# A two-layer streaming encoder step on one core: layer C's channel projection for two tiles at once with split operands, and taps behind the scan in every second unit

## The reference, cut to what matters

```python
h = rms_norm(x, rms_g)                       # x * rsqrt(mean(x*x)) * g
z, xbc, dt = _split(h @ w_in, SPLIT_C)       # 2048, 3072 and 32 columns
xbc, new_conv = causal_conv(xbc, conv_state, conv_w, conv_b)   # 4 taps along the rows, per channel
xbc = jax.nn.silu(xbc.astype(F32))
xs, Bm, Cm = _split(xbc, (D_INNER_C, G_C * N_C, G_C * N_C))
y, S = ssd_scan(xs, Bm, Cm, dt, A, S0)       # chunked scan, state carried from chunk to chunk
y = y + d_skip[..., None] * xs
y = y.reshape(B, L, G_C, D_INNER_C // G_C) * jax.nn.silu(z)
y = rms_norm(y, g_y) ; return x + y @ w_out, S, new_conv
```

## Time and profile before

| what | before |
|---|---|
| median of 3 runs | 3149.06 us (3145.97 to 3149.65) |
| the profiled execution | 3149.56 us, span 3147.8 us |
| granted TensorE clock, mean | 0.974 |
| busy: PE, DVE, ACT | 2924.8, 1870.8, 1411.4 us |
| layer C (1250 to 2764 us of the span): PE, DVE, ACT busy | 1451.5, 1225.1, 802.6 us |

### The profile page before, as it was taken

How to read it: one execution, slowest core, us unless ns; L and a number is a source line. 1 busy time by engine, 2 the same in 40 slices (tenths; PEclk the granted TensorE clock), 3 DMA queues, 4 the chain that set the end, 5 groups by cost and what they waited for, 6 DMA issues and landing times. The chain is left out here.

```text
span 3147.8 us, 50003 instructions
## 1 busy us (share of the span) xinstructions
PE 2924.8 (93%) x18074; PEld 2485.2 (79%) x18074; DVE 1870.8 (59%) x4798; ACT 1411.4 (45%) x2901; POOL 67.9 (2%) x167
## 2 busy tenths in 40 slices
PE   6999996888888986899999999999999999889999
PEld 3798985676766764799988999799997999768787
DVE  3344444444444443588887888788887888832322
ACT  3555555333333332355555555555554555431211
POOL 0000001000000000000000000000000000000000
PEclk9999998999999998899999999999999999889999
DMA  5122223122222211521214221322223212154343
GB/s 191 70 86 85 85 85 134 59 72 85 85 84 85 84 65 56 183 62 57 66 51 132 67 66 56 90 89 67 67 63 104 60 58 67 44 187 141 126 140 114
DMA packets 147547, 280.86 MB, mean 89 GB/s; under 512 B 46231, under 2 KB 69274, under 8 KB 143226
## 3 DMA queue, kind: packets, MB, share of 16 engines
q1 hardware_dynamic: 145458, 274.12, 26.5%
q10 hardware_dynamic: 1992, 5.48, 0.4%
HBM read 204.29 MB, written 75.26 MB: 89 GB/s over the span
## 5 line engine op out<-in xcount | busy, mean ns | idle before, releaser
L2065 PEld LDWEIGHTS bank<-hT_c,w_group 128*128 128x128 f32 x6528 | 750.0, 192 | 39.7 <-issue 34.0
L2065 PE MATMUL bank<-hT_c,w_group 128*128 128x128 f32 x6528 | 751.3, 275 | 0.0
L1889 DVE SCALAR_TENSOR_TENSOR conv_acc<-u,convw,conv_acc 128x128 f32<-128x128 f32 (+1 forms) x1224 | 331.1, 338 | 10.4 <-ACT conv_acc L1823 8.0
L2052 PE MATMUL bank<-wz_high,h_high 128*128 128x512 f32 (+1 forms) x544 | 240.0, 441 | 12.9 <-DVE wz_low L1970 12.9
L2290 PE MATMUL bank<-wout_high,yT_high 128*128 128x512 f32 (+1 forms) x544 | 212.4, 390 | 6.6 <-DVE wout_low L2259 6.6
L2052 PE MATMUL bank<-wz_low,h_high 128*128 128x512 f32 (+1 forms) x544 | 215.9, 397 | 0.0
L2052 PE MATMUL bank<-wz_high,h_low 128*128 128x512 f32 (+1 forms) x544 | 215.5, 396 | 0.0
L2290 PE MATMUL bank<-wout_high,yT_low 128*128 128x512 f32 (+1 forms) x544 | 212.3, 390 | 0.0
L2290 PE MATMUL bank<-wout_low,yT_high 128*128 128x512 f32 (+1 forms) x544 | 212.2, 390 | 0.0
L710 PE MATMUL bank<-wa_high,hT_high 128*128 128x512 f32 (+5 forms) x544 | 189.6, 349 | 12.1 <-DVE wa_low L567 12.1
L710 PE MATMUL bank<-wa_low,hT_high 128*128 128x512 f32 (+5 forms) x544 | 186.8, 343 | 0.0
(11 more groups left out here) (289 smaller groups left out, 5815.1 us busy)
## 6 DMA issues: line engine op xcount, KB each, us to landing
hT_c<-h1T SPq DMA_DIRECT2D x64, 512.0 KB, 3.3
acb<-acT SPq DMA_DIRECT2D x64, 512.0 KB, 3.3
yT_in<-yT SPq DMA_DIRECT2D x32, 1024.0 KB, 5.1
yT<-yT_t SPq DMA_DIRECT2D x64, 256.0 KB, 3.5
xin<-in_x_prompt SPq DMA_DIRECT2D x16, 512.0 KB, 3.7
h0T_high_d<-hT_high SPq DMA_DIRECT2D x16, 512.0 KB, 2.6
h0T_low_d<-hT_low SPq DMA_DIRECT2D x16, 512.0 KB, 3.5
h0T_high<-h0T_high_d SPq DMA_DIRECT2D x16, 512.0 KB, 3.5
```

Source lines behind the costliest of these rows:

```text
L1889: ins = V.scalar_tensor_tensor(acc[:, i, 0:R], ub[:, i, tap:tap + R], c["convw"][:, tap * CT + ct:tap * CT + ct + 1], acc[:, i, 0:R], ALU. ...
L2052: ins = M(B_Z[0:x.R, :], h[:, k, 0:x.R], wt[:, k, :], start=(k == 0 and p == 0), stop=(k == KT - 1 and p == 2))
L2065: ins = M(out, wg[x.g % 2][:, k, j * P:(j + 1) * P], hT[x.buf][:, k, :], start=(k == 0), stop=(k == KT - 1))
```

## The change

Layer C's channel projection (x, B and C blocks) is made for a pair of prompt tiles at once. Its operands are split like those of the gate: three fp32r matmuls with 256 moving columns for each block of channels and of the inner dimension, instead of two f32 matmuls with 128 moving columns (one for each tile). The pair's six blocks ("slots": B, C, x0, x1, x2, x3) are made in two halves of three: a unit with an even t makes slots 0 to 2 of the next pair, a unit with an odd t makes slots 3 to 5 of its own pair. The sample's 32 rows ride with the first pair (288 columns). Taps, first tap, tanh and the SiLU product work on three slots of 256 (or 291) columns in each unit that has a half. In units with odd t (and in the sample's) VectorE makes them before the scan, as before; in units with even t the scan comes first and the taps behind it. Units with t = 1 have no half.

h of layer 1 is written by SWA as a high and a low part, without `rms_g`; `rms_g` is multiplied into the weights when they are split. So `low` and ACT's high part of h leave layer C, and in their place both the x/B/C weights (8 blocks of 768 columns) and z's weights (8 of 512) are split for each group, at the ends of the steps of tiles 14 and 15. ACT's half of z goes away: VectorE reads z from PSUM. In SWA the prompt's bias is restored once by a DMA instead of by a GpSimd copy for each tile.

```diff
@@ SWA
-                    V.tensor_tensor(h1T[:, 4 * k:4 * k + 4, 0:R], B_H2[k]..., bc(c["vec"][:, V_RMS1 + 4 * k:...], R), ALU.mult).then_inc(s["h2_half"], 1)
+                    V.tensor_copy(h1T[:, 4 * k:4 * k + 4, 0:R], B_H2[k]...).then_inc(s["h2_copied"], 1)
+                since(dve, s["hT_out"], x, 1, 32)
+                for k in range(2):
+                    dve.wait_ge(s["h2_high"], 2 * t + k + 1)
+                    V.tensor_tensor(h1l[:, 4 * k:4 * k + 4, 0:R], h1T[...], h1h[...].bitcast(F32), ALU.subtract).then_inc(s["h2_half"], 1)
+            def x1_high(x):
+                    A(h1h[:, 4 * k:4 * k + 4, 0:x.R], h1T[:, 4 * k:4 * k + 4, 0:x.R], ACT.Copy).then_inc(s["h2_high"], 1)
+                if x.fixed and x.t == 1:
+                    sp.wait_ge(s["sc_added"], 8)
+                    sp.dma_start(bias[:, :, 0:P], d["bprev"]).then_inc(s["bprev_in"], 16)
@@ layer C, TensorE
-                for j in (range(4), range(4, 6))[part]:
-                    out = (B_X, B_BC)[part][:, (j % 4) * P:(j % 4 + 1) * P]
-                    for k in range(KT):
-                        ins = M(out, wg[x.g % 2][:, k, j * P:(j + 1) * P], hT[x.buf][:, k, :],
-                                start=(k == 0), stop=(k == KT - 1))
+            def slot(h, i, out):
+                col = SLOT_W[i]
+                for k in range(KT):
+                    if h.first and i == 0:
+                        pe.wait_ge(s["x_low"], KT * h.g + k + 1)
+                    for p, (y, wt) in enumerate(((hh, xh), (hh, xl), (hl, xh))):
+                        ins = M(out, wt[:, k, col:col + P], y[h.par][:, k, h.h0:h.h0 + h.n], start=..., stop=...)
+                elif part == 0:
+                    slot(h, h.lo, B_U[0][:, 0:2 * P])
+                    slot(h, h.lo + 1, B_U[0][:, 2 * P:4 * P]).then_inc(s["uj_full"], 2)
+                else:
+                    slot(h, h.lo + 2, B_U[1][:, 0:2 * P]).then_inc(s["uj_full"], 1)
-                done(pe, s["xc_made"], cur)
+                pe.wait_ge(s["xc_made"], cur.halves)
@@ layer C, VectorE
             def step(cur, nxt, prv):
+                h = cur.half
+                now = h is not None and h.lo > 0
                 if prv is not None:
                     heads_sum(prv)
                 decays(cur)
-                V.scalar_tensor_tensor(zs[0:R, :], zt[0:R, :], 1.0, zh[0:R, :], ALU.add, ALU.mult)
                 if prv is not None:
                     variance(prv)
-                conv(cur, (2,))
+                if now:
+                    taps(h, (2,))
                 if prv is not None:
                     norm(prv)
-                conv(cur, (1, 0))
-                V.scalar_tensor_tensor(acc[:, :, 0:R], th[:, :, 0:R], 1.0, acc[:, :, 0:R], ALU.add, ALU.mult).then_inc(s["xc_made"], 1)
-                    low(following(nxt))
+                if now:
+                    taps(h, (1, 0))
+                    activated(h)
                 if prv is not None:
-                    turned(prv, two_before(prv))
-                scan(cur, prv)
-                    weights_low(nxt.g + 1)
+                    turned(prv, earlier(prv))
+                scan(cur, prv, nxt)
+                if h is not None and not now:
+                    taps(h, (2, 1, 0))
+                    activated(h)
+                    if nxt.t == NT - 2:
+                        weights_low(nxt.g + 1)
+                    if nxt.t == NT - 1:
+                        gate_weights_low(nxt.g + 1)
+            def taps(h, which):
+                for tap in which:
+                    for i in h.slots:
+                        y = acc[h.par][:, i, h.c0:AW]
+                        ins = V.scalar_tensor_tensor(y, ub[:, i, h.c0 + tap:AW + tap], c["convw"][...], y, ALU.mult, ALU.add)
+            def activated(h):
+                dve.wait_ge(s["x_tanh"], h.v + 1)
+                V.scalar_tensor_tensor(y, th[:, :, h.c0:AW], 1.0, y, ALU.add, ALU.mult).then_inc(s["xc_made"], 1)
+            def gate(x):                       # called in scan, ahead of the addition that waits for sup_full
+                V.scalar_tensor_tensor(z, z, 1.0, B_Z[0:x.R, :], ALU.add, ALU.mult).then_inc(s["zs_made"], 1)
@@ layer C, ScalarE: order in a step
-                first tap (6 x 128), ..., tanh(cur), high(h), tanh and half of z(nxt), copies to u(nxt)
+                first_tap(cur.half) (3 x 256), ..., tanh(cur.half) if odd t, tanh of z(nxt), copies to u(nxt.half), tanh(cur.half) if even t
```

More of the change, by code:

```diff
@@ L1176, in scores @@
                 nk = P + R
-                since(dve, s["bias_set"], x, 1)
                 since(dve, s["pt_full"], x, 1, 2)
+                if not x.sample:
+                    dve.wait_ge(s["bias_set"], 1)
+                if not x.fixed or x.t > 1:
+                    dve.wait_ge(s["bprev_in"], 16)
                 if x.sample:
@@ L1582, in layer_c @@
         xd = sb("xd", [P, GW])
-        zh = sb("z_half", [P, GW])
-        zt = sb("z_tanh", [P, GW])
-        zs = sb("zs", [P, GW])
+        zs = [sb(f"zs{i}", [P, GW]) for i in range(2)]
         yb = sb("yb", [P, GW])
@@ L1612, in __init__ @@
                 self.R = DEC if self.sample else P
-                self.buf = (g + (t if isinstance(t, int) else odd)) % 2
-                self.st_before = 19 * g + (1 if self.sample else t + 2)
[L1618 to L1624, removed]
+                self.buf = (g + ph) % 2
+                self.par = 0 if self.sample or ph in (1, 2) else 1
+                second = ph % 2 == 0
+                self.off = 0 if self.sample else UP - 3 + P * second
+                self.hoff = 0 if self.sample else (0 if self.par else DEC) + P * second
+                self.halves = 16 * g + (2 if self.sample else t if second else t + 1)
+                self.half = None
+                if self.sample:
+                    self.half = Half(g, 16 * g + 1, 1, True, 0)
+                elif self.last:
+                    if g + 1 < GC:
+                        self.half = Half(g + 1, 16 * g + 16, 0, True, 0)
+                elif not (isinstance(t, int) and t == 1):
+                    self.half = Half(g, 16 * g + t, ph % 2, False, 1 if ph in (2, 3) else 0)
+                self.st_before = 19 * g + (1 if self.sample else t + 2)
         def done(eng, sem, x, n=1):
@@ L1629, in done, with earlier @@
                 eng.wait_ge(sem, n * (x.u + 1))
+        def earlier(x):
+            if x is None or x.sample and x.g == 0:
+                return None
+            return Unit(x.g - 1, NT - 1, 0) if x.sample else Unit(x.g, x.t - 1, (x.ph + 3) % 4)
         def steps(eng, start, step, end):
-            start(Unit(0, 0))
+            start(Unit(0, 0, 0))
             for g in range(GC):
[L1636 to L1643, removed]
@@ L1644, in steps @@
-            end(Unit(GC - 1, NT - 1))
+                step(Unit(g, 0, 0), Unit(g, 1, 1), Unit(g - 1, NT - 1, 0) if g else None)
+                step(Unit(g, 1, 1), Unit(g, 2, 2), Unit(g, 0, 0))
+                with eng.Fori(2, 7, 4) as t:
+                    for i in range(4):
+                        step(Unit(g, t + i, (2 + i) % 4), Unit(g, t + i + 1, (3 + i) % 4), Unit(g, t + i - 1, (1 + i) % 4))
+                for t in range(10, NT - 1):
+                    step(Unit(g, t, t % 4), Unit(g, t + 1, (t + 1) % 4), Unit(g, t - 1, (t - 1) % 4))
@@ new lines, in load_tile, with load_pair @@
+            def load_tile(par, col, t, R):
+                for dst, src in ((hh, d["h1h"]), (hl, d["h1l"])):
+                    sp.dma_start(dst[par][:, :, col:col + R].bitcast(F32),
+                                 src[t].rearrange("p (k r) -> p k r", k=KT)[:, :, 0:R]).then_inc(s[f"h_in{par}"], 16)
+            def load_pair(t, par, first):
+                if first:
+                    load_tile(par, 0, 0, DEC)
+                for i in range(2):
+                    load_tile(par, (0 if par else DEC) + P * i, t + i, P)
@@ new lines, in _, with fresh, turned @@
+            tail = lambda k, lo, hi, ct: c["tails"][:, k, :, ct:ct + hi - lo].rearrange("p j c -> p c j")
+            def fresh(g, odd):
+                for lo, hi, ct in parts(g, odd):
+                    copy(ub[:, lo:hi, 0:3], c["convs"][:, :].rearrange("p (j c) -> p c j", j=3)[:, ct:ct + hi - lo, :])
+                nc.gpsimd.memset(ub[:, 3 * odd:3 * odd + 3, DEC + 3:UP], 0.0).then_inc(s["tail_set"], 1)
+            def turned(v, odd):
+                pool.wait_ge(s["conv_made"], v + 1)
+                pool.sem_inc(s["pool_step"], 1)
@@ new lines, in carry @@
+            def carry(odd):
+                copy(ub[:, 3 * odd:3 * odd + 3, DEC + 3:UP], ub[:, 3 * odd:3 * odd + 3, UW - 3:UW]).then_inc(s["tail_set"], 1)
+            for odd in range(2):
+                fresh(0, odd)
+            for g in range(GC):
+                for odd in range(2):
+                    turned(16 * g + odd, odd)
+                    for lo, hi, ct in parts(g, odd):
+                        copy(tail(0, lo, hi, ct), ub[:, lo:hi, DEC:DEC + 3])
```

(33 more changed lines are left out.)

409 lines of the change are left out of this document (218 added, 191 removed).

## The result

The changed kernel takes 3234.97 us (median of 4 runs, 3233.64 to 3236.84) where the kernel before takes 3149.36 us (4 runs, 3145.97 to 3150.16): a ratio of 1.0274, 95% interval 1.0257 to 1.0292. It is slower by 86 us, as forecast; 3208 was forecast, with 3150 to 3240 as the range. The profiled execution has a span of 3231.7 us against 3147.8, so the traces stand 83.9 us apart.

The account below looks back on a forecast made before the run. TensorE bounds the kernel (busy 93%), with VectorE's chain only 1.0 us to spare. From 3149.56, +13.6 (units, group edges, start), +2 (SWA) and +44 (lost clock) give 3209, so 3208 us; range 3150 to 3240.

Parts of the forecast that it names:

- TensorE's part: Layer C's projection: new matmuls at 0.1169 us pitch save 2.29 us per unit; even units take 18.58 us.
- The odd unit: Odd t in layer C: VectorE's single chain makes TensorE stand 4.8 us; next state update at T+23.38.
- The rival of cheap taps: VectorE keeps up: a tap with 256 columns costs nearly as little as with 128 (0.26 us); 3118 us; chance 0.12.
- The clock: TensorE's idling in odd units lowers its clock: 1.73 us lost in nine of ten of 28 units, 44 us.
- The rival that the clock stays: TensorE's wait in odd units comes, but its clock stays: 3165 us; chance 0.13.
- The edges: Layer C's group edges: t = 1 and 2 -18.3, t = 15 +30.2, t = 16 and sample -11.1, start +14 us.
- SWA's 2: In SWA the bias's DMA delays one tile by about 2 us.
- The sum: Whole kernel: 3149.56 + 13.6 + 2 + 44 = 3209 us, set to 3208 for the median.
- the likeliest case: Wait and lost clock in layer C's odd units: 3188 to 3230 us; chance 0.67.
- The new wait: Rival: h's loads, or slower matmuls with 256 columns, add a wait; 3290 us at 0.149 pitch; chance 0.08.
- the cover that I named: h's doubled loads in layer C, 2 MB per pair, have some 40 us and two buffers; cost taken as zero.

Follow-up runs that it names:

- the run with filler: The changed kernel plus 16 needless matmuls on TensorE where it waits, in 24 of the 28 odd units: 3195.63 us, ratio 1.0156.

## Why the prediction was right, and what its sizes were

**TensorE's part.** Right. The even unit takes 18.81 us where 18.58 was said. Consecutive projection matmuls lie 0.1188 us apart (18 of them from 1466.83 to 1468.85) instead of 0.1169, which makes 0.14 of the 0.23.

**The odd unit.** Right, step by step. Nine taps took 3.90 us (3.87 said), three 1.27, six 2.58. The first product starts at T+6.49 (6.5 said), the transposes at T+17.04 (17.15 said). The rival of cheap taps fell there: a tap starts 0.40 us after the one before it (three end after 1.27 us, and one lasts 0.47), and for a kernel no slower it had to be under 0.28, or 0.36 with the clock kept. At full clock the unit takes 23.34 to 23.39 us (the run with filler), and 23.38 was said.

**The clock.** The mechanism was right and the term too small. With the chain at 23.37, the six odd units t = 3 to 13 of group 0 took 24.9 to 25.8 us, 25.33 on average: 1.96 us each, where I took 1.73 x 0.9 = 1.56. In the other groups they averaged 25.26. The 24 units paid 45.9 us together, and t = 15 of the first three groups 2.0 each. The last group's t = 15 paid too (transposes at 1.12 us), how much can't be read apart; with the 1.6 of the forecast for it, all 28 make some 53 us instead of 44. The HAM oscillation of the Trainium skill ("TensorE: Matmul & The Clock Gate"), by which idling in each pass throttles each time anew, agrees with that trace; with three taps ahead of the scan 2.8 us of idling throttled only 8 of 28, and with six, 1.4 us throttled none of the pairs before t = 15. The rival that the clock stays is ruled out by the windows above, and by the run with filler.

**The edges.** The unit t = 15 of the first three groups took 33.1 us (1633.99 to 1667.07); at full clock it would be 31.1 (29.82 with three taps ahead, and 1.31), where 30.4 was said. In the last group it took 24.88; the prediction gives no working for its +1.7 there. wx_low's eight took 7.52 us, 7.0 was said. t = 16 took 21.52 as said; the sample 24.65, not 25.5. The last update followed 16.5 us after the one before, where 14.3 was said, at low clock. Layer C's first state update came at 1327.17, 19.7 us later than before, and I had 16 with SWA's 2: SWA gave 4.7 (layer C's first load is issued at 1260.66 instead of 1255.96), the start 15. The sum also took the length of the first group before, 368.4 us, for three groups; together they took 1103.0, 2.1 less.

**The sum.** The mechanism and its parts came out, and the measured time lies near the upper end of the range (3150 to 3240); the narrower one for the likeliest case, 3188 to 3230, was missed by 5 us. The spans stand 83.9 us apart and the sum gave 59.6, so 24.3 were missed: the clock +9.7, the even units 28 x 0.22 = +6.2, t = 15 +2.9, SWA +2.7, the start +1.0, the last unit +2.3, the samples -2.5, the length of the groups before +2.1. That is 24.4. No step failed; the clock's term was the one most too small, and nearly all the errors have one sign.

**The new wait.** h's loads took 6.0 and 6.9 us to landing instead of 3.3, and TensorE nowhere waits for them inside the groups: the cover that I named held.

**Cause shown or argued.** That the placing of the taps behind the scan costs the time is shown: undone it gives back 175 us (ratio 1.0274 to 0.9719), in parts it gives the parts. That the clock's loss comes of TensorE's idling is shown by the run with filler. SWA's share, and that of the last unit, is read from the trace and not tried by itself. What decides from unit to unit how much of the clock is lost stays open.

## What to carry to other kernels

When an engine's work is moved behind a point at which it waits for another engine, add up everything that stands between that point and the next hand-over, both rounds of it: here VectorE had time to spare (busy for 1106 of the 1600 us of layer C's window, 69%), and the chain of two rounds was longer than TensorE's work of the unit. Work ahead of the wait, where the engine stood idle, was nearly free: the even units stayed at 18.8 us with six taps there and took up to 19.2 with all nine. Then ask what the new gap does to TensorE's clock: here it cost some 53 us of the 175, and needless work in the gap gave back 39 of them.

## What the runs showed of the hardware

- Two waits of one length in one run, 2.77 and 2.89 us, gave different clocks: the shorter one was followed by half the clock (granted 0.51 in the window 1426 to 1429 of the run with three taps ahead), the longer one by full clock (1.00 in 1468 to 1471). The length of the last wait alone doesn't decide.
- In the changed kernel the loss was of two sizes: the odd units t = 3, 5 and 7 took 24.7 to 25.1 us, t = 9, 11 and 13 25.6 to 25.8, in every group. In t = 5 and 7 of the first group the transposes behind the wait still ran at 0.71 and 0.66 us and the clock fell behind them; from t = 9 on they took 1.11 or 1.12 us. What shifts it is open; no run was made for it.
